# Parting the 640 token columns of the float32r split products 192 + 448 instead of 320 + 320

## The reference

```python
def project(h, lp):
    u = h @ lp['w_in']                      # 1024 -> 2304
    q, k_att, v_att, rkv = jnp.split(u, [ATT_Q, ATT_Q + ATT_KV, ATT_Q + 2 * ATT_KV], axis=-1)
...
def swiglu(h, w1, w3, w2):                  # layer 0: 1024 -> 2816 -> 1024
    return (jax.nn.silu(h @ w1) * (h @ w3)) @ w2
```

## Time and profile before

| | us |
|---|---|
| median of the runs (2 runs, 2722.01 both) | 2722.01 |
| the profiled execution's own time | 2724.16 |
| its span, first to last instruction | 2722.3 |
| TensorE matmul busy | 2521.7 (93%) |
| TensorE weight load busy | 2197.1 (81%) |
| VectorE busy | 1401.3 (51%) |
| ScalarE busy | 1128.5 (41%) |
| GpSimd busy | 146.1 (5%) |
| mean granted TensorE clock, share of full | 0.975 |

### The profile page before, as it was taken

How to read it: one execution, slowest core, us unless ns; L and a number is a source line. 1 busy time by engine, 2 the same in 40 slices (tenths; PEclk the granted TensorE clock), 3 DMA queues, 4 the chain that set the end, 5 groups by cost and what they waited for, 6 DMA issues and landing times.

```text
span 2722.3 us, 68039 instructions
## 1 busy us (share of the span) xinstructions
PE 2521.7 (93%) x30324; PEld 2197.1 (81%) x30324; DVE 1401.3 (51%) x2474; ACT 1128.5 (41%) x2126; POOL 146.1 (5%) x163
## 2 busy tenths in 40 slices
PE   6998799898899999989987999998999999999996
PEld 3996577676798999969965777766899999999995
DVE  2337455556533333362374665474565555555565
ACT  3226544544421211242255545444444444444452
POOL 0002000010000000010010010001000000000011
PEclk8999899999999999999998999998999999999998
DMA  7223023320122222222200222202765666566672
GB/s 273 78 78 127 24 74 96 96 75 27 70 77 72 78 78 78 72 72 78 78 11 1 66 66 66 65 5 109 240 209 178 214 212 207 183 211 211 181 259 83
DMA packets 82701, 304.58 MB, mean 112 GB/s; under 512 B 9376, under 2 KB 9504, under 8 KB 82272
## 3 DMA queue, kind: packets, MB, share of 16 engines
q1 hardware_dynamic: 71072, 257.93, 29.6%
q0 software_dynamic: 11328, 42.21, 4.2%
HBM read 273.11 MB, written 27.00 MB: 110 GB/s over the span
## 4 chain that ended last, share of the span: by engine, by line
PE 83%; DVE 8%; issue 3%; ACT 3%; DMA 1%; POOL 0%; SPq 0%; another core or an unknown queue 0%; DVEq 0%; ACTq 0%; POOLq 0%
PE ps L451 19%; PE ps L452 19%; PE ps L453 19%; PE ps L1183 7%; PE ps L812 3%; PE ps L917 2%; PE ps L464 2%; PE ps L1115 2%; PE ps L960 1%; PE ps L976 1%; DMA ring<-in_blocks 1%; PE ps L463 1%; DVE arena L2474 1%; DVE arena L2473 1%; PE ps L1167 1%
## 5 line engine op out<-in xcount | busy, mean ns | idle before, releaser
L2278 DVE TENSOR_TENSOR ring_lo<-ring,w_ffn 128x1024 fp32r<-128x1024 f32 x264 | 322.5, 1225 | 214.5 <-ACT w_ffn L1702 208.5
L451 PE MATMUL ps<-hg_hi,w_ffn 128*128 128x256 f32 x1408 | 402.5, 286 | 3.2 <-DVE hg_lo L2909 3.2
L452 PE MATMUL ps<-hg_lo,w_ffn 128*128 128x256 f32 x1408 | 398.0, 283 | 0.0
L453 PE MATMUL ps<-hg_hi,ring_lo 128*128 128x256 f32 x1408 | 397.5, 282 | 0.0
L1702 ACT ACTIVATE w_ffn<-ring 128x1024 fp32r<-128x1024 f32 x264 | 278.1, 1057 | 197.7 <-PE ps L453 196.2
L451 PEld LDWEIGHTS ps<-hg_hi,w_ffn 128*128 128x128 f32 x1408 | 267.4, 190 | 4.8 <-DVE hg_lo L2909 3.4
L452 PEld LDWEIGHTS ps<-hg_lo,w_ffn 128*128 128x128 f32 x1408 | 266.5, 189 | 1.2
L453 PEld LDWEIGHTS ps<-hg_hi,ring_lo 128*128 128x128 f32 x1408 | 267.0, 190 | 0.0
L1183 PEld LDWEIGHTS ps<-arena 64*64 64x64 f32 x7680 | 165.0, 135 | 98.1 <-issue 78.5
L453 PE MATMUL ps<-hT_ffn_hi,ring_lo 128*128 128x320 f32 x704 | 216.0, 307 | 0.0
L1183 PE MATMUL ps<-arena 64*64 64x64 f32 x7680 | 190.5, 222 | 22.6 <-issue 22.2
(11 more groups left out here) (375 smaller groups left out, 5107.1 us busy)
## 6 DMA issues: line engine op xcount, KB each, us to landing
ring<-in_blocks SPq DMA_DIRECT2D x484, 512.0 KB, 3.7
h_rows<-arena POOLq DMA_DIRECT2D x16, 512.0 KB, 10.2
arena<-h_rows POOLq DMA_DIRECT2D x7, 1024.0 KB, 9.9
y_rows<-arena POOLq DMA_DIRECT2D x7, 1024.0 KB, 6.6
x<-in_x_all SPq DMA_DIRECT2D x1, 2560.0 KB, 13.2
h_plain<-arena POOLq DMA_DIRECT2D x1, 2560.0 KB, 11.6
out_y_all<-x POOLq DMA_DIRECT2D x5, 512.0 KB, 3.7
w<-in_low POOLq DMA_DIRECT2D x2, 768.0 KB, 6.4
```

The lines of the kernel that those rows point to most:

```text
L451: nc.tensor.matmul(dst, w_hi, m_hi, start=start, stop=False)
L452: nc.tensor.matmul(dst, w_hi, m_lo, start=False, stop=False)
L453: return nc.tensor.matmul(dst, w_lo, m_hi, start=False, stop=stop)
L2278: V.tensor_tensor(ring_lo[:, n % RING, :], ring[:, n % RING, :], high[:, n % high.shape[1], :], ALU.subtract).then_inc(*E.sig("w_lo"))
```

## The change

`mm640_split` cuts the 640 columns at 192 instead of 320, so each call issues three matmuls with 192 columns and three with 448. `pair_r` moves up by 128 columns, to 320 to 960 of the pair, so that the cut again falls on the bank edge at 512. Number and order of instructions, operands, waits and signals are otherwise as before.

```diff
@@ -444,7 +444,7 @@
         def pair_r(n):
 
-            return pair(n)[:, 192:832]
+            return pair(n)[:, 320:960]
...
         def mm640_split(nc, n, w_hi, w_lo, h_hi, h_lo, start, stop):
-            for h in range(2):
-                sl = slice(320 * h, 320 * h + 320)
+            for sl in (slice(0, 192), slice(192, T)):
                 mm = mm_split(nc, pair_r(n)[:, sl], w_hi, w_lo, h_hi[:, sl], h_lo[:, sl], start, stop)
             return mm
```

## The result

The changed kernel takes 2768.93 us (median of two runs, 2767.86 and 2769.99) against 2722.01 before: a ratio of 1.0172, with a 95% interval of 1.0129 to 1.0216. The forecast was 2770 with a range of 2720 to 2800. A second set, five runs of the changed kernel against fifteen of the kernel before on the same chip, gave 1.0190 (1.0162 to 1.0217); it stands with the experiments. So the change costs 1.7 to 1.9%, 47 to 54 us; both intervals reach past 1.02, so on which side of 2% the cost lies is left open. One execution of all those behind this document, of the kernel with the change in the feed-forward alone, took 4116.10 us at a mean granted clock of 0.553; it stands outside the ratios.

What follows compares the result with a forecast made beforehand. The prediction took TensorE's matmul stream as the bound: 664 calls in it, each 71 ns dearer (three matmuls at 111 ns, three at 201), add 47 us to 2722.0, giving 2769, stated as 2770 us, range 2720 to 2800.

Steps and rivals of the forecast that it cites:

- What bounds the kernel: Feed-forward and projection windows: a pure TensorE matmul stream, 688 calls of six matmuls at 144.3 ns, 596 us, 22%.
- Three matmuls of 192 columns at 111 ns: Narrow part of each call: held by the 4-byte weight load at 111 ns, saving 33 ns each against 144.3.
- The upper bound of 120: Narrow matmul spacing: at most 120 ns, possibly what a float32r load costs in a stream.
- Three matmuls of 448 columns at 201 ns: Wide part of each call: bound by streaming its columns, 201 ns each, between 197.6 and 204.3.
- The upper end, 204.3: Wide matmul spacing: upper bound of 204.3 ns, on the line from 320 columns to the 512-column stream.
- Sum of a call: One call of six matmuls: 936 ns instead of 866, 70 to 71 ns more; 664 calls in the stream give 47 us.
- Calls hidden in the norm stages: 24 calls in three norm stages: the added 0.07 us each falls into a gap and costs nothing; uncovered, 1.7 us.
- The PSUM view, readers, DMAs: Moved PSUM view, ScalarE and VectorE readers, weight DMAs: no cost and no prefetch gained; SyncE's waits only lengthen.
- The signs named: Changed timeline: three spacings near 111, three near 201 ns; feed-forward window 83.1 to 89.9 us; stretches without 640-column products unchanged.
- rival A: Matmul stream: loads pulled further ahead stay hidden, narrow 91 ns, wide 197.6, call 866, time 2722 us; chance 0.12.
- B: Narrow matmuls: float32r loses its single pass, four passes per product, call 1608 ns, about 3230 us; chance 0.15.
- C: Matmul stream: slower float32r load, 120 and 204.3 ns, call 973 ns, 2796 us; top of the load-bound case (0.68).

Runs made afterwards that it cites:

- the halved load: The changed kernel (192 + 448), with narrow matmuls loading only 64 of 128 weight columns in six of eight calls per block: 2739.38 us, 1.0094.
- the alternating kernel: The changed kernel (192 + 448), with narrow and wide matmuls alternating instead of three and three: ratio 1.0195 to the kernel before.

## Why the prediction was right

*What bounds the kernel.* Right. The long stretches of 640-column products grew by 50.3 us where the medians grew by 47 and 54, and halving the number of changed calls halved it.

*Three matmuls of 192 columns at 111 ns.* Right: 108, 111 and 112, mean 110. The value came from the turn of modulation rows, a plain float32 load, and held for float32r. The cut at 128 shows the same 110, and the halved load shows that it is the load. The upper bound of 120, read from the 256-column stream, was no price of a load: in the kernel with the 256 + 384 cut, 256 columns take 117 to 119 ns while a load takes 110. The Trainium skill, "TensorE: Matmul & The Clock Gate", section LDWEIGHTS, has the time of a load grow with its columns, and the halved load agrees in direction; the estimate from its formula, 106.7 ns for 128 columns, is some 4 ns under the mean measured.

*Three matmuls of 448 columns at 201 ns.* Mis-sized: 205. I took the middle between a fixed surplus of 11 ns per matmul and the line to the 512-column stream. The upper end, 204.3, was nearly it: a float32r column costs about 0.46 ns in all of these streams, so the surplus over 1/2.4 grows with the columns. That is 4 ns on three matmuls, 12 ns per call by the means of the long stretches (205, 209 and 201, which hold the few waits too).

*Sum of a call.* 936 predicted, 943 inside a stretch, +77 instead of +71: 664 x 6 ns = 4 us more than said. The measured growth of the long stretches is 50.3 us where 47 was the forecast. That the first comparison gave just 47 is in part luck: the scans vary by some us from one execution to the next, and the 2722.01 us of the two runs of the kernel before lie 4 us over the median of its fifteen later ones. The larger set gave 53.6.

*Calls hidden in the norm stages.* Put at nothing, and not quite nothing. The trace before and the second trace of the changed kernel had the same granted clocks in the three stages (1.00, 0.85 and 1.00). From the first 640-column product of a stage to the start of the long stretch behind it, five calls on, they took 9.53, 11.09 and 9.51 us before and 9.73, 11.33 and 9.72 us after: 0.65 us more over 15 calls, 43 ns a call where 71 would be the whole. So the gaps hide part of the cost only. Over all 24 calls that is an estimate of 1 us, too little to see in the time of a run.

*The PSUM view, readers, DMAs.* Nothing of them shows in the windows or the chain, as forecast.

*The signs named.* They were to be read from start to start in the timeline. Read from the matmul starts, the first narrow spacing is 0.08 us, near rival A's 91 ns, and the first wide one 0.22, over the 205 allowed. Only the load starts give three spacings near 111 and three near 201. The stretches without 640-column products did not keep their lengths in the first trace; the second trace showed that the change was not the cause. The window of 576 loads grew to 90.5 us where 89.9 was forecast.

*Rivals.* A, the load hidden all the same, is out: it asked for narrow gaps of 91 ns and no loss. The apparent 86 ns gap in the matmul rows made me believe a part of it for one experiment, and the alternating kernel took that away. B, four passes below some width, is out: at 192 and at 128 columns there is one matmul row per product and the mean gaps under it stay at 108 to 112 ns. C, the upper edge, had the wide term right and the narrow one wrong.

## What to carry to other kernels

A stream in which each matmul has its own weight load costs, per matmul, the larger of its columns (here 0.46 ns each) and the next load (here 110 ns for 128 columns of 4 bytes): a cut of a fixed number of columns should leave no part under that break-even, an estimate of 240 columns from these two figures (256 columns were clear of the load, 192 were not), and the even cut is the safe one. Where one part fell below it, neither a narrower cut nor another order helped; shorter loads did, and fewer loads were not tried. To see what such a stream costs, take the distances between load starts and not those between matmul rows.

The 110 ns belong to a granted clock of 1.00, the 2.4 GHz level. In the trace of the kernel before, a later turn of modulation rows, the same loads as in the earlier trace rows, ran at a granted clock of 0.50, the 1.2 GHz level, and from one load start to the next it has 213 ns (the median):

```profile
39.51 1.57 PEld L820 LDWEIGHTS ps<-con,modrow 128*128 128x128 f32 x7 [1.66 <-issue]
39.50:41.00 1.50, 1.49 (x8) 0.50 1.07 426
```

So at the lower clock the load is nearly twice as dear.

## What the runs showed that was not expected

A matmul's row can begin 82 to 91 ns after its load began, though the next load starts only 110 ns after it, and the row is then some 20 ns longer (0.39 against 0.37 and 0.36 us above). With 128 columns in the narrow part it begins sooner still, 54 to 61 ns after: about when the matmul before it has streamed its columns, whatever its own load does. This looks like overlap and gains nothing, as the alternating kernel shows.

The kernel before is at a small optimum of its own: three and three matmuls on an exactly even cut cost 870 ns per call, and moving the cut by 8 columns, or alternating the halves, costs 10 to 13 ns, 0.3% of the time with intervals that leave out 1. Its cause is open.
